# Expert weights as pairs of neighbouring rows, one 8 KB piece per partition

## What is computed

```python
for l in range(2):
    sh1, sc1, g1, sh2, sc2, g2 = split(silu_c @ w_mod[l] + b_mod[l], 6)
    hx = modulate(rmsnorm(x_lat, norm1_g[l]), sh1, sc1)
    x_lat = x_lat + g1 * token_mixer(hx, hc, ...)          # in projection, four mixers, gates, out projection
    hx2 = modulate(rmsnorm(x_lat, norm2_g[l]), sh2, sc2)
    x_lat = x_lat + g2 * ec_moe(hx2, router_w[l], w1[l], w3[l], w2[l])
    # layer 0 does the same for the context tokens; layer 1 does not
return rmsnorm(x_lat, final_g)

def ec_moe(h, router_w, w1, w3, w2):                       # 16 experts, each takes its 32 best tokens
    aff = softmax(h @ router_w)
    gate, idx = top_k(aff.T, 32)
    xs = h[idx]
    hid = silu(xs @ w1[e]) * (xs @ w3[e])                  # each of w1, w3, w2: 1024 x 1024 per expert
    y = hid @ w2[e] * gate
    # rows of y are added back at idx
```

## Time and profile before

| | us |
|---|---|
| median of 3 runs | 2217.62 (2214.98 to 2222.05) |
| the profiled execution, its own time | 2219.25 |
| its span | 2217.4 |
| PE busy (matmul / weight load) | 1888.8 / 1129.9 |
| VectorE (DVE) busy | 699.1 |
| ScalarE (ACT) busy | 444.5 |
| GpSimd (POOL) busy | 109.2 |
| mean granted TensorE clock | 0.949 of full speed |
| bytes moved | 562.64 MB, 318,024 packets |

### The profile page before, as it was taken

The page is one execution under the profiler, slowest core; times in us unless marked ns, Lnnn a source line. Parts: engine busy times, 40 slices in busy tenths (PEclk is TensorE's granted clock), DMA queues, the critical chain, the costliest instruction groups (busy, mean ns, idle before and its releaser), DMA issues.

```text
span 2217.4 us, 25119 instructions
## 1 busy us (share of the span) xinstructions
PE 1888.8 (85%) x10106; PEld 1129.9 (51%) x10106; DVE 699.1 (32%) x1114; ACT 444.5 (20%) x792; POOL 109.2 (5%) x150
## 2 busy tenths in 40 slices
PE   6999999999999699999999899999997655555554
PEld 3888766666777533333233388877886211111111
DVE  2272354333334512221122454554455100001001
ACT  2322333222222310000000332443333000000000
POOL 1070000000000000000000231000000000000000
PEclk9999999999999799999999999999999788888887
DMA  9423234234446489999999862443687899999996
GB/s 296 118 77 101 84 101 125 75 100 124 143 142 236 167 335 409 410 410 410 409 410 409 269 164 87 127 124 113 181 239 289 344 409 409 409 409 410 410 409 256
DMA packets 318024, 562.64 MB, mean 254 GB/s; under 512 B 11964, under 2 KB 208620, under 8 KB 317932
## 3 DMA queue, kind: packets, MB, share of 16 engines
q1 hardware_dynamic: 315564, 554.11, 68.4%
q0 software_dynamic: 1824, 5.12, 1.3%
q10 hardware_dynamic: 544, 2.10, 0.2%
HBM read 560.24 MB, written 1.05 MB: 253 GB/s over the span
## 4 chain that ended last, share of the span: by engine, by line
PE 67%; DMA 18%; SPq 7%; DVE 5%; issue 1%; ACT 1%; POOL 0%; POOLq 0%; DVEq 0%; ACTq 0%
PE PS L662 46%; PE PS L1066 14%; SPq L640 7%; DMA e_wr<-in_moe_w 6%; DMA arena<-in_moe_w 6%; DMA nab<-in_moe_w 5%; PE PS L721 2%; PE PS L1017 2%; PE PS L856 1%; PE PS L727 1%; DMA ring<-in_w_mod 1%; DVE wr L1480 0%; PE PS L737 0%; DVE arena L1523 0%; DVE arena L1774 0%
## 5 line engine op out<-in xcount | busy, mean ns | idle before, releaser
L662 PE MATMUL PS<-hTr,wr 128*128 128x512 f32 (+1 forms) x2688 | 516.0, 348 | 5.8 <-DVE hTr L1511 5.8
L662 PEld LDWEIGHTS PS<-hTr,wr 128*128 128x128 f32 x2688 | 428.4, 190 | 74.0 <-issue 10.9
L1066 PE MATMUL PS<-arena 128*32 128x512 f32 (+1 forms) x960 | 297.0, 689 | 102.5 <-DMA nab<-in_moe_w 52.0
L1480 DVE TENSOR_TENSOR wr<-ring,wr 128x1024 fp32r<-128x1024 f32 x152 | 187.7, 1236 | 226.8 <-ACT wr L1132 226.7
L1132 ACT ACTIVATE wr<-ring 128x1024 fp32r<-128x1024 f32 x152 | 160.6, 1057 | 297.0 <-PE PS L662 279.8
L1066 PE MATMUL PS<-e_h,arena 128*64 128x512 f32 (+1 forms) x624 | 161.8, 675 | 60.0 <-DMA arena<-in_moe_w 54.2
L1066 PE MATMUL PS<-arena,e_h 128*64 128x512 f32 (+1 forms) x576 | 162.0, 670 | 45.6 <-DMA e_wr<-in_moe_w 24.4
L1066 PEld LDWEIGHTS PS<-arena 128*32 128x32 f32 (+1 forms) x960 | 80.6, 138 | 227.2 <-issue 222.2
L662 PE MATMUL PS<-wr,hTr 128*128 128x512 f32 x816 | 189.5, 393 | 4.2 <-DVE wr L1480 2.2
L662 PEld LDWEIGHTS PS<-wr,hTr 128*128 128x128 f32 x816 | 153.2, 189 | 38.0 <-DVE wr L1480 3.2
L1858 DVE TENSOR_TENSOR x<-x,PS 128x512 f32<-128x512 f32 x80 | 55.0, 688 | 258.2 <-PE PS L662 258.2
(11 more groups left out here) (169 smaller groups left out, 1938.2 us busy)
## 6 DMA issues: line engine op xcount, KB each, us to landing
arena<-in_moe_w SPq DMA_DIRECT2D x192, 1024.0 KB, 18.2
e_h<-in_moe_w SPq DMA_DIRECT2D x90, 1024.0 KB, 18.2
ring<-in_w_in SPq DMA_DIRECT2D x136, 512.0 KB, 4.6
e_wr<-in_moe_w SPq DMA_DIRECT2D x64, 1024.0 KB, 18.3
ring<-in_w_mod SPq DMA_DIRECT2D x96, 512.0 KB, 6.1
nab<-in_moe_w SPq DMA_DIRECT2D x32, 1024.0 KB, 18.4
ring<-in_w_br SPq DMA_DIRECT2D x64, 256.0 KB, 5.6
ring<-in_w_out SPq DMA_DIRECT2D x16, 512.0 KB, 4.4
```

The lines of the kernel that those rows point to most:

```text
L662: return nc.tensor.matmul(o, a, b, start=first, stop=last)
L1066: ins = nc.tensor.matmul(PS[g * R:(g + 1) * R, bank + h, :], src[:, k, g * R:(g + 1) * R], space[:, kk * D + h * 512:kk * D + (h + 1) * 51 ...
L1480: nc.vector.tensor_tensor(wr[:, j % 2, 1, :], ring[:, slot, :], wr[:, j % 2, 0, :].bitcast(f32), ALU.subtract).then_inc(w_lo.sem, 1)
```

## The change

Row pairs take the place of block pairs. A group of 256 rows is laid over the partitions so that partition p gets rows 2p and 2p + 1, which are neighbours in memory, in one piece of 8 KB. The first row of each pair is then "block" r = 0 and the second r = 1. Everything that has to be in the same order follows: the new function `paired(v, k)` takes for block k every second column of 256, and it is the source of the transposes of the tokens, of the hidden values and of the second norm; `mod_post` takes every second column of `modp` for parts 3 and 4 (second norm's shift and scale); the second norm's gains and the router's weights are laid out on the host in the same order. Slots, waits and the number of transfers stay.

```diff
+def paired(v, k):
+
+
+    return v.rearrange("t (j p r) -> t j r p", p=128, r=2)[:, k // 2, k % 2, :]
...
-            experts = [A[n].rearrange("l e (k p) n -> l (e k) p n", p=128) for n in ("moe_w1", "moe_w3", "moe_w2")]
+            experts = [A[n].rearrange("l e (j p r) n -> l (e j) p (r n)", p=128, r=2)
+                       for n in ("moe_w1", "moe_w3", "moe_w2")]
...
-                                src = w[l, ds(i * (G * KD) + (g * KD + 2 * j), 2), :, :].rearrange("k p n -> p k n")
+                                src = w[l, ds(i * (G * 4) + (g * 4 + j), 1), :, :].rearrange("k p n -> p (k n)")
...
-                                    sync.dma_start(xspace[extra].rearrange("p (k n) -> p k n", k=2), src)\
+                                    sync.dma_start(xspace[extra], src)\
...
-                                    sync.dma_start(espace[s].rearrange("p (k n) -> p k n", k=2), src)\
+                                    sync.dma_start(espace[s], src)\
...
-                        i = mm(PS[:, 7, col:col + 2], modp[:, n % 2, c * 128:(c + 1) * 128],
+                        half_row = modp[:, n % 2, c::2] if part > 2 else modp[:, n % 2, c * 128:(c + 1) * 128]
+                        i = mm(PS[:, 7, col:col + 2], half_row,
...
                         for j in range(2):
+                            k = 2 * kp + kk
+                            row = xn[:, 2 * s + j, :]
                             i = nc.tensor.transpose(PS[:, 4 * s + kp, kk * T + j * 128:kk * T + (j + 1) * 128],
-                                                    xn[:, 2 * s + j, (2 * kp + kk) * 128:(2 * kp + kk + 1) * 128],
-                                                    ident)
+                                                    paired(row, k) if nn % 2 else row[:, k * 128:(k + 1) * 128], ident)
...
-                                                      toks[:, (4 * bk + k4) * 128:(4 * bk + k4 + 1) * 128], ident)
+                                                      paired(toks, 4 * bk + k4), ident)
...
-                                                      hid[:, k * 128:(k + 1) * 128], ident)
+                                                      paired(hid, k), ident)
...
+    pairs = lambda v: np.ascontiguousarray(v.reshape(PQ, 128, 2).transpose(1, 0, 2).reshape(128, KD))
...
-        par[l, :, P_RW:P_RW + KD * E] = a["router_w"][l].reshape(KD, 128, E).transpose(1, 0, 2).reshape(128, KD * E)
+        par[l, :, P_RW:P_RW + KD * E] = a["router_w"][l].reshape(PQ, 128, 2, E).transpose(1, 0, 2, 3).reshape(128, KD * E)
...
-        stay[:, S_N2 + KD * l:S_N2 + KD * (l + 1)] = cols(a["norm2_g"][l], KD)
+        stay[:, S_N2 + KD * l:S_N2 + KD * (l + 1)] = pairs(a["norm2_g"][l])
```

## The result

The changed kernel takes **2191.78 us** (median of 4, 2189.97 to 2195.57) against 2219.84 us for the kernel before (median of 4: the three runs of the prediction's median and a fourth of 2223.51 us). The ratio is 0.9869, with a 95% interval from 0.9856 to 0.9882: 28 us, or 1.3%, less. 2191 was forecast. The profiled execution took 2190.71 us, with a span of 2188.9 us against 2217.4.

What follows compares the result with a forecast made beforehand. Both expert stages were taken to end by the DMA's rate, the first bound by PE until 941 us. 354 paced transfers at 76 ns less gave -26.9 us, other terms 0: 2217.62 to 2190.7 us, range 2184 to 2198 (0.70).

Steps and rivals of the forecast that it cites:

- Which resource ends each stage: Both expert stages end by the DMA's rate; in the first, PE starts to wait about two passes later.
- The cost per piece: Expert-weight transfers: about 9.4 ns per piece beyond its bytes, so 310.6 ns per 8 KB piece, 76 ns less per transfer.
- The smaller cost per piece: Rival for expert transfers: joining pieces saves only 4.3 ns each, 34 ns a transfer; -12 us, 2206; chance 0.08.
- The paced volume: Expert stages: 177 of 192 transfers per layer go at the DMA's pace, so each layer gains 13.4 us.
- PE's room: First expert stage: PE waits 20.0 us, DMA gains 13.4, so PE stays 6.6 us ahead and the whole gain comes through.
- SP: Issue of expert transfers: 384 issues before and after, not the limit; with half the pieces it only runs further ahead.
- The strided loads: PE's weight loads for transposes and modp, now every second float: taken as 0 extra, at most 140 ns each.
- A slower load shows in full: PE's transposes: eight run in 1.09 us, 136 ns each, so they go at the pace of their loads.
- The rivals with half and a third of the rate: Strided PE loads: half rate gives +1.4 us, 2219, chance 0.09; a third gives +36 us, 2254, chance 0.07.
- The sum: Whole kernel: -26.9 us from 354 paced transfers, taking the median of 2217.62 us to 2190.7.

Runs made afterwards that it cites:

- e3: Changed kernel with the two rows of a partition apart in SBUF in 11 of 12 slots, so pieces of 4 KB: 2218.25 us.
- e4: Kernel before with each 4 KB row of expert weights fetched as two pieces of 2 KB: 2271.82 us, ratio to before 1.0231.
- e2: Kernel before with only the changed kernel's strided reads, transfers still in 4 KB pieces: 2220.03 us, ratio to before 0.9999.
- e8: Kernel before with the transposes of tokens and hidden values issued twice in each pass: 2218.84 us, ratio to before 0.9991.
- e7: Changed kernel with the transposes of tokens and hidden values issued twice in each pass: 2202.69 us.
- e7b: Changed kernel with the transposes of tokens and hidden values issued twice, measured a second time: 2199.55 us against 2191.82 beside it.
- e5: Changed kernel with SP waiting so that no more than seven expert transfers are under way: 2194.07 us, ratio to before 0.9882.
- e6: Changed kernel with transposes of tokens reading every 4th float and those of hidden values every 8th: 2192.27 us.

## Why the prediction was right, and where it was not

**Which resource ends each stage.** Right in both. The DMA enters the first stage's chain two passes later, as said.

**The cost per piece.** Right. It is the term that carried the sum: 310.6 ns forecast, 310.9 measured; 2.485 us per transfer forecast, 59.65/24 = 2.485 measured. It came from pieces of 512 B to 4 KB in other stages of the kernel, and e3 and e4 show that it was the cause and not something that came with it. The smaller cost per piece, a rival at 0.08, is excluded by this, and the step between sizes leaves 9.3 ns. The Trainium skill (DMA: Bandwidth & Descriptors, "Why small descriptors are slow") has about 3 cycles of fixed overhead per packet, an estimated 3.5 ns at the page's 850 MHz. The 9.3 ns measured are more than that, so here it can't be the whole cost of a piece.

**The paced volume.** 177 transfers per layer and 13.4 us each were forecast. From the issue of the first paced transfer to the landing of the last, the second layer took 458.4 us before (1737.32 to 2195.70) and 444.8 in the changed kernel (1722.98 to 2167.73): 13.6 us less. The first took 458.4 (788.57 to 1246.97) and 446.2 (786.66 to 1232.86): 12.2 less. One reading of the prediction is wrong here and does no harm: 177 x 2.56 = 453 us is not "what lies between those times", which is 458.4. Some 5 us more lie between them with 8 KB pieces too (444.8 against 177 x 2.485 = 439.8), so they drop out of the difference.

Counted from the first expert matmul to the last, the second stage went from 470.0 to 454.0 us, but 467.1 to 467.2 us is what it takes in e2, e3 and e8, which have 4 KB pieces in all or 11 of 12 slots; by these the gain is 13.1 us. The other 2.8 us belong to the one execution of before that was traced. In 1.7 of them its first slot came free later, 5.35 us after the first expert matmul (1731.97 to 1737.32 us) where e2 and e8 took 3.65: from 1731 to 1736 us its granted clock was 0.72, so part of the time at the lower of the two levels (1.2 GHz), and in e2 it was 1.00 (2.4 GHz). The remaining 1.1 us were not traced to a cause.

The first stage went from 467.6 to 455.4 us, 12.2 in place of 13.4. From 815 to 830 us (columns as in the stretches above) the changed kernel shows this:

```profile
815.00:820.00 5.00, 5.00 (x34) 3.27 (x34) 4.32 (x10) 2.48 (x3) 0.00 (x0) 1.00 1.01 421
820.00:825.00 5.00, 5.00 (x26) 1.70 (x24) 0.10 (x1) 0.00 (x0) 0.00 (x0) 1.00 0.68 256
825.00:830.00 5.00, 5.00 (x26) 1.59 (x24) 0.00 (x0) 0.00 (x0) 0.00 (x0) 1.00 1.00 418
```

The DMA runs dry at 820 us, while SP waits for PE to free slots behind the gather and the transposes (9.3 us at one slot after, 9.1 before). It moved 256 GB/s in these 5 us, where the kernel before moved 307: a faster DMA waits longer where PE has not freed its slots yet. Against their full rates of 422 and 410 GB/s, that is an estimated 5 x (166/422 - 103/410) = 0.7 us of the missing 1.2; the rest was not traced to a cause.

**PE's room.** Right: 6.6 us forecast, 6.0 us measured as waits, and e7 and e7b show that extra PE work beyond it costs time.

**SP.** Right: SP's part of the chain went from 7% to 1%, and e5 shows that this is no part of the gain.

**The strided loads.** The term was 0 and measured 0.21 us per pass. In the first stage PE's waits cover that, and what the uncovered ones cost (the second norm's, those of modulation and the first tokens of a layer) is too small to show: e2 has them all and its interval ends at 1.8 us. So the sum did not notice. The reasoning behind it failed in two places. "A slower load shows in full", because eight transposes took 136 ns each and a load 140, was wrong: the record of a load grew by 69 ns and the pace by 13. The 136 ns were 1.09/8, which counts the last transpose's whole length; e8 shows that one more transpose costs 110 ns, so the transposes of before did not go at the pace of their loads to begin with. And the load at stride one was not the right neighbour for a load at stride two, whose record is 209 ns. The rivals with half and a third of the rate did not come: no load tried took more than 1.5 times as long on record. The Trainium skill (SBUF — State Buffer, the note on cachelines) would have had strides of up to 4 floats free, and a penalty where each access meets a new line, as at 8. The records of e6 and the changed kernel differ from that: all three strides are above stride one (209, 209 and 193 ns against 140), with 8 the cheapest of the three.

**The sum.** -26.9 us forecast, -28.1 us by the medians (26 to 32 by the interval of the ratio). The spans of the two traces differ by 28.5 us: 12.2 in the first stage, 15.9 in the second, and 0.4 elsewhere. Of these the 2.8 us of the second stage above are not shared by e2, e3 and e8, so what the traces tie to the pieces is 12.2 + 13.1 = 25 us. The other 1 to 3 us of the medians' difference stay open; in the runs of one kernel alone the time moves by more than that, and what makes an execution slower was not traced. That the time itself, 2191.78 us, came out within 1 us of the forecast is partly luck: with the fourth run the median of before was 2.2 us higher than the 2217.62 that the forecast started from, and the gain was 1.2 us larger, which nearly cancel.

## What to carry to other kernels

Where a stage runs with a full DMA, divide engine time by pieces for every piece size the trace already has; if the points lie on a line, its value at the new size is the forecast, and joining rows so that a partition gets one longer piece is worth (pieces saved per engine) x (the line's constant) x (paced transfers). Then check how much the other engine still waits by the end of the stage, as a sum: in a stage of few passes like this one (eight) that is the cover there is, both for the gain and for extra work, and the lengths of the two engines' passes side by side don't tell it. And count the transfers that leave before the first slot is freed: where the stage ends by the DMA, each one more is worth about a transfer time (two gave 4.6 us here).

## What the runs showed of the hardware that was not expected

At a granted clock of 1.00, the load of a transpose's source (128 floats in each of 128 partitions) is recorded at 140 ns when the floats are adjacent, at 209 ns at a stride of 2 and of 4 floats, and at 193 ns at a stride of 8, but eight transposes with such loads take only 1.12 to 1.23 us instead of 1.04 to 1.09. At 0.50 it is 227 ns adjacent and 224 ns at a stride of 2. One more transpose costs 110 ns with a load of 140 on record (e8), and e7b's sixteen in 2.11 and 1.92 us, against 1.15 and 0.96 for eight in the changed kernel's chain, make it 120 ns with a load of 209. The length of a load's record is thus no measure of what it adds to the pace of the matmuls around it.

With 4 KB pieces SP was held at seven transfers of 1 MB under way (18.2 us from issue to landing, 18.2/2.56 = 7.1); with 8 KB pieces a transfer in the chain took up to 25.9 us from issue to landing, and SP's share of the chain fell from 7% to 1%; with 2 KB pieces the median fell to 14.2 us, five transfers (14.2/2.71 = 5.2). The rate did not depend on it: 422 GB/s at seven under way (e5) and at more.
